# First RWKV pair's decay, key and receptance features made in the input projection's last block and in the attention, with multiplications by GpSimd

## What is computed

```python
for d, (wd, ad) in enumerate(((wf, af), (wb, ab))):
    w_log = -jax.nn.softplus(-(lp['w0'][d] + jnp.tanh(wd) @ lp['w2'][d])) - 0.5
    a = jax.nn.sigmoid(lp['a0'][d] + ad @ lp['a2'][d])
    decays.append(_heads(jnp.exp(-jnp.exp(w_log))))
    ks.append(_heads(k * (1.0 + (a - 1.0) * lp['ka'])))
    iclrs.append(_heads(a))
```

## Time and profile before

| | us |
|---|---|
| median of 3 runs (lowest to highest) | 1749.96 (1747.49 to 1757.27) |
| profiled execution, its own time | 1752.18 |
| span of that execution | 1750.4 |
| busy: PE / PEld | 1608.0 / 1326.3 |
| busy: DVE / ACT / POOL | 707.9 / 564.6 / 857.5 |
| mean granted TensorE clock | 0.954 of full |

### The profile page before, as it was taken

How to read it: one execution, slowest core, us unless ns; L and a number is a source line. 1 busy time by engine, 2 the same in 40 slices (tenths; PEclk the granted TensorE clock), 3 DMA queues, 4 the chain that set the end, 5 groups by cost and what they waited for, 6 DMA issues and landing times. The chain is left out here.

```text
span 1750.4 us, 35639 instructions
## 1 busy us (share of the span) xinstructions
PE 1608.0 (92%) x15692; PEld 1326.3 (76%) x15692; DVE 707.9 (40%) x1062; ACT 564.6 (32%) x809; POOL 857.5 (49%) x397
## 2 busy tenths in 40 slices
PE   5899999687888888989999999999989999999996
PEld 3688878566686876868888888888867788888885
DVE  1333246677675754552121212640284521212135
ACT  3423245543434322233232323132222432323230
POOL 1432200197968552437888888744442344444441
PEclk9999899899999999989999999969989799999998
DMA  7321100021312122214444344212221122222221
GB/s 311 125 74 71 58 1 1 1 99 62 126 57 105 52 100 80 73 48 145 146 145 145 143 146 145 90 48 96 96 96 49 48 96 97 96 96 96 96 96 48
DMA packets 23618, 162.17 MB, mean 93 GB/s; under 512 B 2624, under 2 KB 3264, under 8 KB 4800
## 3 DMA queue, kind: packets, MB, share of 16 engines
q1 hardware_dynamic: 21904, 154.09, 24.6%
q10 hardware_dynamic: 1584, 6.13, 0.9%
HBM read 157.71 MB, written 2.10 MB: 91 GB/s over the span
## 5 line engine op out<-in xcount | busy, mean ns | idle before, releaser
L221 POOL TENSOR_TENSOR v<-raw,v 128x1024 fp32r<-128x1024 f32 x160 | 389.6, 2456 | 420.7 <-ACT v L209 396.1
L238 PE MATMUL bank<-hm,v 128*128 128x512 f32 x2112 | 488.3, 393 | 7.4 <-DVE hm L1895 5.1
L238 PEld LDWEIGHTS bank<-hm,v 128*128 128x128 f32 x2112 | 399.4, 190 | 96.8 <-issue 10.4
L238 PE MATMUL bank<-hid,v 128*128 128x512 f32 x1536 | 349.5, 389 | 0.0
L238 PEld LDWEIGHTS bank<-hid,v 128*128 128x128 f32 x1536 | 288.3, 188 | 59.9
L209 ACT ACTIVATE v<-raw 128x2048 fp32r<-128x2048 f32 x77 | 147.5, 1916 | 420.9 <-PE bank L238 420.8
L2026 DVE TENSOR_TENSOR bank<-bank,rl 128x512 f32<-128x512 f32 x64 | 44.8, 700 | 275.1 <-ACT rl L2005 275.1
L221 POOL TENSOR_TENSOR w<-raw,w 128x1024 fp32r<-128x1024 f32 x22 | 54.2, 2485 | 137.0 <-ACT w L209 137.0
L940 POOL TENSOR_TENSOR raw<-raw,cs 128x2048 f32<-128x2048 f32 x24 | 87.0, 3627 | 52.8 <-DVE at L1395 52.8
L511 PE MATMUL bank<-h,w 128*128 128x512 f32 x600 | 109.1, 344 | 0.0
L511 PEld LDWEIGHTS bank<-h,w 128*128 128x128 f32 x600 | 93.7, 191 | 14.4 <-issue 0.3
(11 more groups left out here) (298 smaller groups left out, 2332.6 us busy)
## 6 DMA issues: line engine op xcount, KB each, us to landing
raw<-w_in SPq DMA_DIRECT2D x119, 1024.0 KB, 4.8
mraw<-wm_in SPq DMA_DIRECT2D x16, 1024.0 KB, 4.8
raw<-wm_in SPq DMA_DIRECT2D x3, 1024.0 KB, 16.4
xres<-x_in ACTq DMA_DIRECT2D x1, 2048.0 KB, 9.0
yb<-wm_in SPq DMA_DIRECT2D x2, 1024.0 KB, 19.9
mixed_in<-wm_in SPq DMA_DIRECT2D x2, 1024.0 KB, 23.4
xres<-x_in SPq DMA_DIRECT2D x1, 2048.0 KB, 8.9
out_T<-xres ACTq DMA_DIRECT2D x8, 256.0 KB, 2.0
```

The lines of the kernel that those rows point to most:

```text
L221: i = nc.gpsimd.tensor_tensor(W[1][n % 2][:, k:k + 4], raw[n % 2][:, k:k + 4], W[0][n % 2][:, k:k + 4].bitcast(F32), SUB)
L238: last = nc.tensor.matmul(bank(b(s, m), 0, hi - lo), W[w][s][:, k, m * P:(m + 1) * P], H[h][:, k, lo:hi], start=(k == 0 and w == h == 0), ...
```

## The change

Nothing is computed otherwise; the features of pair 0 are made earlier and partly on another engine. The eight LoRA products of pair 0 stand in the middle of the projection's last block, behind its third of eight slices. ScalarE makes the tanh and the eight sigmoids there, before it copies out the last tile, into the two `raw` buffers (called `sigma`). In the attention ScalarE makes the scaled keys behind units 2 and 3, the exponentials behind units 8, 9, 12 and 13, and the reversed values behind units 27 and 28. VectorE makes the cumulative sums in eight quarters behind units 2 to 9. GpSimd makes all products of pair 0, also those that VectorE did: key products, key sum, products with Pn, decayed keys and receptance. Only the second bs operation of pair 0 stays at the start of RWKV, on VectorE. SP loads the first two modulation blocks in the attention, once the `raw` buffers are free. To have room, the attention's probabilities and outputs lie in the RWKV tiles AM, XT and MT, `Rp` and `msum` in the attention's constants, and `g2` in the LoRA weights.

```diff
@@ projection, SP: two loads fewer @@
-                with sp.Fori(0, (NB - 1) // 2) as turn:
+                with sp.Fori(0, (NB - 3) // 2) as turn:
@@ projection, TensorE, in in_turn behind slice k @@
+                            if n == S_MOD - 1 and k == 2:
+                                lora_pieces()
+                def lora_pieces():
+                    pe.wait_ge(later_in, 16 * PAIRS)
+                    pe.wait_ge(tile_free[(S_MOD - 2) % 2][1], nth(S_MOD - 2))
+                    pe.wait_ge(tanh_ready, 1)
+                    for i, (kind, seg, d) in enumerate(PIECES):
+                        if i == 3:
+                            pe.wait_ge(knormed, PAIRS)
+                        if i == 4:
+                            pe.wait_ge(mixed, 14)
+                        if i == NP - 1:
+                            pe.wait_ge(sig_ready, 1)
+                        lo, hi = SEG[seg]
+                        r = slice(d * HD, (d + 1) * HD)
+                        nc.tensor.matmul(bank(LORA_BANK[i], 0, hi - lo), lw[r, 0, kind, :], lora[r, kind, lo:hi],
+                                         start=True, stop=True).then_inc(lora_done, 1)
@@ projection, ScalarE, called before tile 20 is copied @@
+                def gates():
+                    act.wait_ge(mixed, 13)
+                    nc.scalar.activation(lora[:, 0, :], lora[:, 0, :], ACT.Tanh).then_inc(tanh_ready, 1)
+                    for s in range(2):
+                        act.wait_ge(split_ready[(S_MOD - 1 - s) % 2], nth(S_MOD - 1 - s))
+                    for i, (kind, seg, d) in enumerate(PIECES):
+                        lo, hi = SEG[seg]
+                        act.wait_ge(lora_done, i + 1)
+                        o = sigma[kind][:, d, lo:hi]
+                        nc.scalar.activation(o[:, ::-1] if d else o, bank(LORA_BANK[i], 0, hi - lo), ACT.Sigmoid,
+                                             bias=R("a0" if kind else "w0", 4 * d, 4 * d + 1)).then_inc(sig_ready, 1)
@@ attention, SP and GpSimd @@
+                sp.wait_ge(kp_ready, 1)
+                sp.wait_ge(bb_ready, 1)
+                sp_load(sp, S_MOD)
+                sp.wait_ge(cum_ready, 2)
+                sp_load(sp, S_MOD + 1)
+            def _(pool):
+                nc.gpsimd.memset(Pp[:].rearrange("p d n j -> p (d n) j")[:, :, 0:1], 1.0)
+                pool.wait_ge(kp_ready, 1)
+                for d in range(2):
+                    for k, lo, hi in in_order(d, kT[:, 0, :]):
+                        i = nc.gpsimd.tensor_tensor(KTL[:, d, lo:hi], KTL[:, d, lo:hi], k, MUL)
+                i.then_inc(kpk_ready, 1)
+                for d in range(2):
+                    for k, lo, hi in in_order(d, kkT[:, 0, :]):
+                        i = nc.gpsimd.tensor_tensor(BT[:, d, lo:hi], sigma[1][:, d, lo:hi], k, MUL)
+                i.then_inc(bb_ready, 1)
+                pool.wait_ge(kpk_ready, 1)
+                nc.gpsimd.tensor_tensor(bs[:], KTL[:, 0, C:N], KTL[:, 1, C:N][:, ::-1], ADD).then_inc(ksum_ready, 1)
+                pool.wait_ge(decay_ready, 4)
+                pool.wait_ge(ksum_ready, 1)
+                nc.gpsimd.tensor_tensor(KTL[:], KTL[:], Pn[:], MUL).then_inc(prod_ready, 1)
+                pool.wait_ge(bb_ready, 1)
+                nc.gpsimd.tensor_tensor(BT[:], BT[:], Pn[:], MUL).then_inc(prod_ready, 1)
+                ... (PC's copy, three products for AT_, two for RT)
@@ attention, ScalarE, behind each unit @@
+                    if u in (2, 3):
+                        d = u - 2
+                        act.wait_ge(ones_ready, 1)
+                        i = nc.scalar.activation(KTL[:, d], sigma[1][:, d], ACT.Identity, scale=R("ka", 0, 1),
+                                                 bias=oka[:, 0:1])
+                    if u in (8, 12):
+                        d = (u - 8) // 4
+                        act.wait_ge(cum_ready, d + 1)
+                        nc.scalar.activation(Pp[:, d, :, 1:Q + 1], AT_[:, d, :].rearrange("p (n j) -> p n j", j=Q),
+                                             ACT.Exp, scale=-DECAY).then_inc(decay_ready, 1)
+                    if u in (9, 13):
+                        nc.scalar.activation(Pn[:, d, :], AT_[:, d, :], ACT.Exp, scale=DECAY).then_inc(decay_ready, 1)
@@ attention, VectorE, behind units 2 to 9 @@
+                    d, n = i // 4, N // 4
+                    lo = (i % 4) * n
+                    j = nc.vector.tensor_tensor_scan(AT_[:, d, lo:lo + n], K("scan", lo, lo + n),
+                                                     sigma[0][:, d, lo:lo + n], 0.0, MUL, ADD)
@@ RWKV: taken out at its start @@
-            for i in range(NP):
-                lora_piece(0, i)
-            for i in range(NP):
-                gate(0, i)
-            keys(0)
-            exponentials(0, 0)
-            exponentials(0, 1)
-            reversed_values(0)
-            cumulate(0, 0)
-            cumulate(0, 1)
-            features(0)
-            receptance(0)
+            nc.vector.scalar_tensor_tensor(bs[:], bs[:], R("rk", 0, 1), rT[:, 0, :], MUL, MUL).then_inc(bs_ready, 1)
```

More of the change, by code:

```diff
@@ L583, in _ @@
                             continue
+                        if t == 20:
+                            gates()
                         act.wait_ge(tile_done[n % 2][m], nth(n))
@@ L731, in _ @@
                         transposed(u - 1)
-                nc.scalar.activation(lora[:, 0, :], lora[:, 0, :], ACT.Tanh)
+                    first_pair(u)
                 nc.scalar.activation(gT[:], gT[:], ACT.Sigmoid)
@@ L838, in _ @@
                         output(u - 1)
+                    if 2 <= u < 10:
+                        decay_sums(u - 2)
                 output(NU - 1)
@@ L893, in build @@
     NDVE = len(ORDER) - NACT
-    PIECES = [(kind, seg, d) for kind in range(2) for seg in range(2) for d in range(2)]
-    SEG = ((0, C), (C, N))
-    NP = len(PIECES)
     def half(i):
@@ L976, in lora_piece @@
                 r = slice(d * HD, (d + 1) * HD)
-                if p and i:
+                if i:
                     pe.wait_ge(sig_ready, NP * p + i)
-                nc.tensor.matmul(bank(7 if p else i, 0, hi - lo), lw[r, p, kind, :], lora[r, kind, lo:hi], start=True, stop=True)\
+                nc.tensor.matmul(bank(7, 0, hi - lo), lw[r, p, kind, :], lora[r, kind, lo:hi], start=True, stop=True)\
                     .then_inc(lora_done, 1)
@@ L1259, in gate @@
                 act.wait_ge(lora_done, NP * p + i + 1)
-                if p and i == 0:
+                if i == 0:
                     act.wait_ge(b_done, p)
                 o = (BT if kind else AT_)[:, d, lo:hi]
-                nc.scalar.activation(o[:, ::-1] if d else o, bank(7 if p else i, 0, hi - lo), ACT.Sigmoid,
+                nc.scalar.activation(o[:, ::-1] if d else o, bank(7, 0, hi - lo), ACT.Sigmoid,
                                      bias=R("a0" if kind else "w0", 4 * d + p, 4 * d + p + 1)).then_inc(sig_ready, 1)
@@ L1550, in build @@
     rw_sb.close()
+    att_in.close()
     one = ((lambda s, m: 2 * s + m, (0, T)),)
```

140 lines of the change are left out of this document (86 added, 54 removed).

## The result

The changed kernel takes 1800.08 us (median of 4 runs, 1794.68 to 1806.19), the kernel before 1753.62 us beside it (4 runs, 1747.49 to 1758.11). The ratio is 1.0268, with an interval of 1.0215 to 1.0321. The forecast was 1735. The profiled execution took 1803.0 us, 50.8 more than the one of before.

What follows compares the result with a forecast made beforehand. The prediction saw one long sequence of stages, with a serial chain of 20.3 us before RWKV that nothing hides; -20.3 - 2.0 + 2.9 + 4.5 - 0.1 = -15.0 gave 1737.2 profiled, 1735.0 median; range 1729 to 1743.

Steps and rivals of the forecast that it cites:

- the price of a delay past the slack: Attention: VectorE's delays less slack, 2.9 us in GpSimd's first burst, 0.5 in its second; 7.8 if L815 is held too.
- a granted clock that sinks in the attention: One of the signs listed as showing the prediction wrong, to be seen in the attention of the profile after.
- rival (c): Attention units with GpSimd work: the lock serializes GpSimd and the loop, at most 22.8 us, 1753.4 in all; chance 0.03.
- whether a one-column instruction is held: Attention, L821 and L815 on VectorE: left open whether GpSimd's instructions delay them; cost 0, 3.4 or 7.8 us.
- The chain, -20.3: Between attention and RWKV: pair 0's unhidden serial feature chain, from LoRA products to first transposes, goes, saving 20.3 us.
- Cold start and mask, -2.0: RWKV's start: without half clock and receptance products, VectorE's first mask comes 2.3 instead of 4.3 us after the transposes.
- pair 0, -0.1: RWKV's pair 0 behind its start: GpSimd's later modulation products cost 0.9 us, a shorter scan wait gives -1.0.
- The projection, +2.9: Projection's last block: the eight LoRA products lengthen it by 2.9 us, range 2.5 to 4.5; ScalarE's gates are covered.
- The attention, +4.5: Attention: GpSimd's products delay VectorE's SBUF instructions and so TensorE; ends 0 and 7.8 us, taken as +4.5.
- Slack, 1.7 us: Attention unit: the delay in VectorE or ScalarE that can pass before TensorE stands, about 1.7 us.
- Rival (b): Attention: VectorE held twice a unit, extra exponentials meet delayed maxima, +10; gates uncovered, +1.5; 1741 or 1744 us; chance 0.13.

Runs made afterwards that it cites:

- a_den: Changed kernel with the attention's denominator sum (L821) written as a scalar operation, one SBUF tensor and a pointer: 1738.0 us against 1755.5 before, ratio 0.9908.
- a_dveprod: Changed kernel with GpSimd's attention products made by VectorE in 13 pieces behind units 10 to 22: 1737.3 us.
- a_best3: Changed kernel with the scalar-form denominator sum, scaled keys behind units 10 and 11, two keep-warm products at the projection's end: 1735.5 us against 1751.4, ratio 0.9905.
- a_nodma: Changed kernel with SP's two weight loads in the attention moved behind GpSimd's last product: 1801.6 us against 1751.4 for the kernel before.
- a_warm3: Changed kernel with one 512-column keep-warm product of TensorE in each of attention units 4, 5 and 6: 1737.1 us against 1751.4 before.
- b_stall: Kernel before with two ScalarE copies added in the attention, 2560 columns behind unit 4 and 2048 behind unit 6: 1747.4 us against 1757.6.
- b_one: Kernel before with one ScalarE copy of 3840 columns added behind attention unit 4: 1819.0 us against 1751.3, ratio 1.0386.
- b_stall3: Kernel before with ScalarE copies of 3840 and 2816 columns behind attention units 4 and 5: 1820.3 us against 1751.4; timed again, 1826.1 us, ratio 1.041.
- a_kick: Changed kernel with eight 512-column keep-warm products of TensorE in attention unit 16 alone: 1772.4 us against 1757.6 for the kernel before.
- b_stall2: Kernel before with two ScalarE copies of 3840 columns, behind attention units 4 and 6: 1754.6 us against 1755.5.

## Why the prediction was wrong

**What failed** is one step: "the price of a delay past the slack". The prediction counted what VectorE's delays leave beyond the slack once, at face value: 2.9 + 0.5 = 3.4, or 7.8. The delay came, and near that size: 0.68 + 1.17 = 1.85 us of stops. What it left out is that these stops cost the granted clock, and the loop can't win it back: 161.9 us of attention where 96.6 + 1.85 and 1.7 for the slow start (below) would be 100.2, so 61.7 of the 65.3 us. The prediction named "a granted clock that sinks in the attention" as what would make it wrong, yet gave it neither a price nor a chance, and its rival (c), the slower one, was another mechanism, capped at GpSimd's own 22.8 us. The rows to price it were there: the earlier trace rows show TensorE idle, then 1.54 us for six transposes that take 0.87 at full clock. From them the rival reads: a unit of 2.83 us becomes up to 1.77 times as long (1.54 / 0.87), 5.0 us, for the 27 units behind the burst, up to 59 us. Measured: 5.1 us a unit (five of them from 300.95 to 326.53) and 61.7 us. How small a stop suffices no row of before showed; its trace even has a pause of 2.59 us at full clock, in front of the first scores:

```profile
233.19 0.71 PE L745 MATMUL bank<-xres,yb 64*128 64x256 f32 x4 [2.59 <-PEq L483]
```

But a mechanism with a price of 60 us beside a gain of 15 belonged among the rivals, with the time 1735 + 59 = 1794, and the range ended 51 us below it.

**L821 held.** The question that the prediction left open, "whether a one-column instruction is held", is answered: L821 is, up to 2.78 us where it took 0.15; L815 never is. What decides at one column is the form of the instruction, two SBUF tensors against one and a pointer, shown by a_den with the same sum in the other form. It isn't the number of SBUF inputs alone at every width: L2096, a scalar operation with one SBUF tensor of 512 columns, takes 0.49 or 2.26 us. The Trainium skill's rule in "SBUF — State Buffer", section "SBUF: two separate sides", gave this rightly, at one column too; the +4.5 was a middle between it and the rest, and the held case, 3.4, was nearest, for the stops alone.

**The rest of the sum held**, part by part, and a_den shows it. That its profiled execution took 1736.4 us, where the prediction for the changed kernel's profile was 1737.2, is in part luck: the parts that the prediction has a term for make -16.2 (-20.0, -1.8 behind it, +3.9, +1.7) against -15.0, and two stretches for which it has none, up to the last projection block (-2.4) and behind the output stage (+2.8), nearly cancel.

- *The chain, -20.3*: in a_den the first last copy stands at 332.99 and the transposes at 336.06, 3.07 us, against 23.10 before: -20.0. Right.
- *Cold start and mask, -2.0, and pair 0, -0.1*: the first mask comes 1.8 us after the transposes instead of 4.3 (-2.5); at the output stage -1.6 is left (-1.8 in a_den). GpSimd begins its modulation products at 406.99, 4.7 us behind the block's start (the prediction took 3 for its semaphores), and TensorE's stage gave back some of it. Right in sum: -1.6 against -2.1. The full clock that the -2.0 counts on isn't sure: in a_dveprod and a_best3 the second six transposes take 1.54 us again, and in a_nodma the first six 1.51.
- *The projection, +2.9*: +3.9, alike in four kernels (the changed one, a_den, a_warm3 and a_best3: 12.23 or 12.24 us from last block to first scores). The eight products take 3.74 us, not 2.85: they wait for the gates' banks, and a table load (1.28 us at 227.69) stands before the gates. Within its range, 1 us low.
- *The attention, +4.5*: in a_den 98.3 us against 96.6, and this 1.7 is not the lock. The eight dense products at the attention's start take 5.40 us instead of 3.70, since the clock was at 0.50 for 3.5 us there, which comes and goes between executions of either kernel (last section); in a_best3, without it, the attention takes 96.6. So GpSimd's and VectorE's added work costs nothing in itself, end 0 of the range, once the sum isn't held.
- *Slack, 1.7 us*: too small on ScalarE, where b_stall's 2.34 us left under 0.2 and a copy of 3.41 stopped TensorE for 1.03 to 1.04: some 2.4. VectorE's wasn't measured.
- *Rival (b)*: its own terms (+10 and +1.5 in place of +4.5) make -8.0, or 1742, and not -9.3. Nothing else rests on it.

```profile
235.75 5.40 PE L174 MATMUL bank<-cst 128*128 128x512 f32 x8
```

## What to carry to other kernels

Before adding a delay to a loop that just keeps TensorE dense, ask for the granted clock beside the slack: a single stop of 1 us in one unit cost 68 us here, because the loop keeps a full clock but didn't win it back once it had fallen. Price it as a rival of its own (what is left of the stage, times what half clock makes of it), and look at the clock's line before explaining a longer stage by waits. An elementwise sum of two SBUF columns is held by GpSimd's work for as long as a wide one; written with the second column as a scalar pointer it isn't, for 0.05 us more.

## What the runs showed of the hardware

- **The fall.** In the attention's loop, otherwise dense, stops of 0.64 us and less never cost the clock in a trace, nor did a first stop of 0.67 to 0.69. One of 1.03 to 1.04 us did in three of four traces, and with the executions that have a time alone in ten of eleven; one of 1.16 to 1.19 us, behind one of 0.68, in all three traces. The fall came within the stop (b_one, b_stall3) or behind its end: 0.8 us in a_nodma, 1.0 in b_stall3_timed, 1.7 in the changed kernel.
- **No regaining.** With TensorE's records nearly back to back the clock stayed at 0.50 for 136 us in the changed kernel; eight products of 512 columns brought it to 1.00 (a_kick), as they do at the attention's start. It also came back within a run of transposes and small products (358.0 in the kernel before) and behind one of transposes (401.8 in the changed kernel); what the loop lacks isn't shown.
- **The moment has a part.** The pause between projection and attention is the same, 2.59 us, in b_stall3 and b_stall3_timed, one kernel in two executions: in the first the clock stays at 1.00 and eight products take 3.70 us, in the second it falls for 3.5 us and they take 5.40. The same pause stands in 18 of the 20 traces, and the clock fell behind it in nine of them. The Trainium skill, "TensorE: Matmul & The Clock Gate", section "Part 1: The HAM clock gate", says that the watching of activity runs free of the kernel, so that the moment of a change varies from run to run; these two executions agree. It may be the reason of b_stall2's exception too, which wasn't tried; b_one's five executions all went one way.
- **The lock.** GpSimd's products held `den` up to 2.78 us and scans of 192 columns up to 1.90, and never a one-column operation with one SBUF input (L960, 213 to 217 ns in 32 units).
